# Both output projections start inside the block before them, and the router's choices are made a few tiles at a time

## What is computed

```python
# layer 0: all 1280 tokens; layer 1: only the latents go on after the mixer
h  = modulate(rmsnorm(x, norm_g[l,0]), shift, scale)       # six modulation rows per layer, from c and c_ctx
o  = neighbourhood_attention(h)  if l == 0 else  rglru_mixer(h)      # both end in "@ w_o + b_o"
x  = x + gate * (o @ w_o + b_o)                            # the projection
h2 = modulate(rmsnorm(x, norm_g[l,1]), shift2, scale2)
# hier_moe(h2): group logits (4), top 1; expert logits (8 in the group), top 2; softmax weights;
# 32 experts with SwiGLU of width 512; weighted sum over the two experts of each token
x  = x + gate2 * hier_moe(h2)
```

## Time and profile before

| | us |
|---|---|
| median of 3 runs (lowest, highest) | 2957.16 (2955.74, 2960.85) |
| the profiled execution | 2956.72 |
| its span, first to last instruction | 2954.9 |
| PE busy | 2611.4 (88%) |
| PE weight loads busy | 1813.8 (61%) |
| DVE, ACT, POOL busy | 1068.0, 859.6, 478.5 |

### The profile page before, as it was taken

How to read it: one execution, slowest core, us unless ns; L and a number is a source line. 1 busy time by engine, 2 the same in 40 slices (tenths; PEclk the granted TensorE clock), 3 DMA queues, 4 the chain that set the end, 5 groups by cost and what they waited for, 6 DMA issues and landing times. The chain is left out here.

```text
span 2954.9 us, 68818 instructions
## 1 busy us (share of the span) xinstructions
PE 2611.4 (88%) x28080; PEld 1813.8 (61%) x28081; DVE 1068.0 (36%) x2350; ACT 859.6 (29%) x1860; POOL 478.5 (16%) x590
## 2 busy tenths in 40 slices
PE   7999999999879749999999489999859599999990
PEld 6787778787635437777777344454425477777770
DVE  3233333434434322222222546556453322222225
ACT  3222322222300013333333424333400033333333
POOL 0111111111211012222222300000011022222222
PEclk9999999999979879999999589999979699999995
DMA  6323223222273467999999510000072699999995
GB/s 247 114 91 115 92 98 128 78 94 85 94 258 104 152 266 314 417 416 397 416 416 360 203 58 29 28 28 28 0 258 86 267 361 417 416 417 416 416 389 178
DMA packets 145570, 646.14 MB, mean 219 GB/s; under 512 B 33632, under 2 KB 45920, under 8 KB 89520
## 3 DMA queue, kind: packets, MB, share of 16 engines
q1 hardware_dynamic: 107600, 541.50, 46.6%
q0 software_dynamic: 17984, 57.16, 5.6%
q10 hardware_dynamic: 19872, 45.84, 4.1%
HBM read 579.86 MB, written 64.57 MB: 218 GB/s over the span
## 5 line engine op out<-in xcount | busy, mean ns | idle before, releaser
L1247 PE MATMUL PS<-wt,xT 128*32 128x256 f32 x13056 | 751.5, 381 | 32.6 <-DVE xT L1414 19.8
L1247 PEld LDWEIGHTS PS<-wt,xT 128*32 128x32 f32 x13056 | 512.5, 110 | 232.1 <-issue 41.0
L1262 PE MATMUL PS<-wt,hidT 128*32 128x256 f32 x6528 | 395.2, 379 | 3.5 <-ACT y L1155 3.5
L1155 ACT ACTIVATE y<-PS 32x256 f32<-32x256 f32 x816 | 306.3, 375 | 304.2 <-PE PS L1262 296.9
L1414 DVE STREAM_TRANSPOSE xT<-xg 128x256 f32<-128x256 f32 x206 | 91.8, 446 | 670.9 <-PE PS L1247 653.6
L1262 PEld LDWEIGHTS PS<-wt,hidT 128*32 128x32 f32 x6528 | 256.6, 110 | 99.5 <-issue 4.4
L691 PE MATMUL PS<-hT,slab 128*128 128x256 f32 x1280 | 297.1, 386 | 9.1 <-DVE low L589 6.3
L691 PEld LDWEIGHTS PS<-hT,slab 128*128 128x128 f32 x1280 | 240.5, 193 | 46.4 <-DVE low L589 8.3
L399 POOL TENSOR_SCALAR prob<-prob,inv 128x640 f32<-128x640 f32 (+2 forms) x80 | 130.4, 1629 | 677.4 <-DVE inv L604 677.4
L1100 POOL DMA_INDIRECT xg<-h_d,ib x212 | 208.3, 983 | 171.6 <-POOL ib L1097 171.6
L484 ACT ACTIVATE prob<-prob,low 128x640 f32<-128x640 f32 (+2 forms) x160 | 117.5, 735 | 293.5 <-DVE low L589 286.8
(11 more groups left out here) (228 smaller groups left out, 2580.3 us busy)
## 6 DMA issues: line engine op xcount, KB each, us to landing
wt<-in_w SPq DMA_DIRECT2D x256, 1024.0 KB, 19.4
wt<-in_w2s SPq DMA_DIRECT2D x128, 1024.0 KB, 18.6
aw<-in_ada_w SPq DMA_DIRECT2D x48, 1024.0 KB, 5.0
ys_d<-y ACTq DMA_DIRECT2D x204, 128.0 KB
slab<-in_slabs SPq DMA_DIRECT2D x24, 512.0 KB, 3.4
tab<-in_tables SPq DMA_DIRECT2D x8, 1408.0 KB, 6.8
ys_d<-zero POOLq DMA_DIRECT2D x4, 2560.0 KB, 11.4
x_d<-x_p ACTq DMA_DIRECT2D x18, 512.0 KB, 5.0
```

Source lines behind the costliest of these rows:

```text
L1155: ins = a.activation(y[rows, q * QD:q * QD + QD], PS[STRIP * q:STRIP * q + STRIP, DOWN, 0:QD], ACT.Copy)
L1247: mm = t.matmul(PS[32 * g:32 * g + 32, UP, 0:QD], xT[:, k * 32:k * 32 + 32], wt[b][:, q, c * 1024 + g * QD:c * 1024 + g * QD + QD], start= ...
L1262: mm = t.matmul(PS[32 * g:32 * g + 32, DOWN, 0:QD], hT_[:, k * 32:k * 32 + 32], wt[b][:, q, c * 1024 + g * QD:c * 1024 + g * QD + QD], sta ...
```

## The change

`projection` becomes a class `Projection` whose parts are called from the attention's and the recurrent layer's block, so two blocks go. Its loops are written out. Its tensors get fixed places, so that its loads can land while the mixer still runs. In outline:

- SP loads `w_o` (four DMAs of 1 MB) at the start of the last head pair (attention), or after the last y product (recurrent). A few steps later come the rows, x and the router's weights, which now lie contiguous in HBM, as one DMA.
- PE computes tiles 0 and 1 without their last k-slice before the mixer's last result is there, in attention between `turn`, `values` and the waits of the last step, and adds the last slice when it is.
- `rows(g)` on DVE runs one step later, after `prob_T`, and `store_mod` with the bias loads moves from ACT to SP, also one step later.
- The gate is applied per half tile. DVE makes the best groups, experts and one-hots for tiles 0 to nt-5 in tile nt-3, for the next two in tile nt-2, and for the last two after the last logits (`choose`), with running sums `A2c` over the tiles.
- In experts, PE needs two products in place of `nt` + 1; the token weights are made while PE sums the indices; and layer 1's columns come as 16 rows of 512 bytes each for latents and context, turned on PE.

```diff
@@ attention, sync
+ if i == STEPS - UNITS:
+     sp.wait_ge(w_ps, NPIECE * PAIRS)
+     pr.load_weights(sp)
+ if i == STEPS - UNITS + ABUF:
+     sp.wait_ge(s_ok, STEPS - UNITS)
...
+     pr.load_first(sp)
...
+ if made is not None:
+     store_mod(made)
+     made = None
...
+ sp.wait_ge(s_ok, STEPS)
+ pr.load_shift(sp)
...
+ sp.wait_ge(on_ok, STEPS)
+ pr.stream(sp)
@@ attention, scalar
- elif n % KD == KD - 1:
-     store_mod(n // KD)
+ pr.scalar(a)
@@ attention, vector
  prob_T(i - 1)
+ if made is not None:
+     rows(made)
+     made = None
  if i < STEPS:
      norm(i)
@@ attention, tensor, after the steps
+ pe.wait_ge(low_ok, 2 * STEPS)
+ pr.weights_ready(pe)
+ pr.part(pe, 0, 0, 0, KD - 1)
+ turn(STEPS - 1)
+ pr.part(pe, 0, 1, 0, KD - 1)
+ values(STEPS - 1)
+ pr.part(pe, 1, 0, 0, KD - 1)
+ pe.wait_ge(on_ok, STEPS)
+ pr.part(pe, 0, 0, KD - 1, KD)
+ pr.part(pe, 0, 1, KD - 1, KD)
+ pr.part(pe, 1, 0, KD - 1, KD)
+ pr.part(pe, 1, 1, 0, KD)
+ pr.rest(pe)
@@ class Projection
+ def part(self, t, n, h, lo, hi):
+     if lo == 0 and n >= 2:
+         t.wait_ge(self.sum1_ok, 3 * (n - 2) + h + 1)
+     for k in range(lo, hi):
+         mm = t.matmul(PS[:, self.banks[n % 2] + h, :], self.Z[:, k, n * P:(n + 1) * P],
+                       self.wo[:, k, h * 512:(h + 1) * 512], start=(k == 0), stop=(k == KD - 1))
...
+ def rest(self, t):
+     H = KD // 2
+     self.part(t, 2, 0, 0, KD)
+     self.turn(t, 0)
+     self.part(t, 2, 1, 0, H)
+     self.route(t, 0)
+     self.part(t, 2, 1, H, KD)
+     self.turn(t, 1)
+     self.part(t, 3, 0, 0, KD)
+     self.route(t, 1)
+     for n in range(2, self.nt):
+         if n > 2 and n + 1 < self.nt:
+             self.part(t, n + 1, 0, 0, KD)
+         if n + 1 < self.nt:
+             self.part(t, n + 1, 1, 0, H)
+         self.turn(t, n)
+         if n + 1 < self.nt:
+             self.part(t, n + 1, 1, H, KD)
+         self.route(t, n)
@@ Projection.vector
+ for n in range(nt):
+     gate(n)
+     if n == 0:
+         for w in range(W):
+             prepare(w)
+     added(n)
...
+     elif n > 2:
+         logits(n - 1)
+     normed(n)
+     if n == 2:
+         logits(1)
+     if n == nt - 3:
+         choose(0, nt - 4)
+     if n == nt - 2:
+         choose(nt - 4, nt - 2)
+ logits(nt - 1)
+ choose(nt - 2, nt)
@@ recurrent, sync
+ sp.wait_ge(u_ps, 2 * LB)
+ sp.wait_ge(y_ps, 2 * LB)
+ pr.load_weights(sp)
+ sp.wait_ge(u_ok, 2 * LB)
+ pr.load_first(sp)
@@ recurrent, tensor, after the loop
+ pr.weights_ready(t)
+ t.wait_ge(y2_ok, 2 * LB + 1)
+ t.wait_ge(z_ok, 2 * LB)
+ pr.part(t, 0, 0, 0, KD - 1)
+ pr.part(t, 0, 1, 0, KD - 1)
+ t.wait_ge(tr_ok, 4 * LB + 1)
+ pr.part(t, 1, 0, 0, KD - 1)
+ pr.part(t, 1, 1, 0, KD - 1)
+ t.wait_ge(z_ok, 2 * LB + 1)
+ for n in range(2):
+     for h in range(2):
+         pr.part(t, n, h, KD - 1, KD)
@@ experts, scalar (layer 0)
- a.dma_start(scol[:, w, :], mod_d[w, ...].rearrange("(k p) -> p k", p=P)).then_inc(cols_in, 16)
- a.dma_start(gcol[:, w, :], mod_d[w, ...].rearrange("(k p) -> p k", p=P)).then_inc(cols_in, 16)
+ a.dma_start(y[2 * KD * w:2 * KD * (w + 1), 0:P], mod_d[w, ...].rearrange("(m p) -> m p", p=P)
+             ).then_inc(cols_in, 16)
@@ experts, tensor
- t.matmul(PS[:, 0, 0:w], ltri[:, :], flat(A2), start=True, stop=False)
- for k in range(nt):
-     mm = t.matmul(PS[:, 0, (k + 1) * EXPERTS:w].rearrange(...), ones[:, :], expand(A2[:, k, :], ...), ...)
+ t.matmul(PS[:, 0, 0:w], ones[:, :], flat(A2c), start=True, stop=False)
+ t.matmul(PS[:, 0, 0:w], ltri[:, :], flat(A2), start=False, stop=True).then_inc(summed, 1)
+ if not last:
+     t.wait_ge(cols_in, 48)
+     t.matmul(PS[:, 5, 0:4 * KD], y[0:4 * KD, 0:P], ident[0:4 * KD, 0:4 * KD], start=True, stop=True
+              ).then_inc(turned, 1)
@@ experts, vector
- v.wait_ge(e_ok, 2)
- link(v.tensor_reduce(gsum, m4, AX, ALU.add))
...
  link(v.tensor_scalar(blk, PS[:, 0, nt * EXPERTS:(nt + 1) * EXPERTS], 1.0 / STRIP, 31.0 / 64, ALU.mult, ALU.add))
...
+ v.wait_ge(e_ok, 2)
+ link(v.tensor_reduce(gsum, m4, AX, ALU.add))
...
  v.wait_ge(summed, 4)
```

More of the change, by code:

```diff
@@ new lines, in attention @@
+                put = Place(nc, PROJ_AT, TOP)
+                early = [put(f"{x}0", [P, w]) for x, w in (("qT", N), ("kT", N), ("V", N))]
+                tab0 = put("tab0", [P, 2, TABW])
+                slab = [put(f"slab{m}", [P, KD, P]) for m in range(3)]
+                qT, kT, Vf = ([x, put(f"{y}1", [P, N])] for x, y in zip(early, ("qT", "kT", "V")))
+                V = [x[:, :].rearrange("p (t c) -> p t c", c=P) for x in Vf]
+                tab = [tab0, put("tab1", [P, 2, TABW])]
+                prob = [put(f"prob{b}", [P, 2, 640]) for b in range(2)]
@@ L283, in attention @@
+                low, sums, inv = (put(x, [P, 2, 2]) for x in ("low", "sums", "inv"))
+                bq = put("bq", [P, 3, PAIRS])
+                zero, cl_ok = put("zero", [P, QD]), gather_sem("ys_cleared")
                 diag = [qT[0][:, j * P:(j + 1) * P] for j in range(2)]
@@ L753, in fill @@
                                     piece(n, i)
-                        for i in range(STEPS + 1):
-                            if i < STEPS:
-                                scores(i)
+                        for i in range(STEPS):
+                            scores(i)
                             if i:
@@ L1005, in experts @@
             nm = lambda s: sem(f"{s}_m{l}")
-            dv, d_ok, e_ok, a_ok, cn_ok, z_ok, t_ok, g_ok, b_ok, o_ok, i_ok = (
-                nm(x) for x in ("dve", "diff", "exp", "assigned", "counts", "order", "tables", "later", "bases", "hot", "index"))
+            dv, e_ok, summed, masks = (nm(x) for x in ("dve", "exp", "summed_on_pe", "masks_made"))
             tab_ok, idx_ok, pad_ok = nm("tab"), nm("idx"), nm("pad")
@@ L1769, in _ @@
                             gates(b, 1, 1)
-        def weights_in(l):
-            return [[sem(f"w{b}{q}_m{l}") for q in range(NCH)] for b in range(WBUF)]
-        with ExitStack() as att:
-            OT = sbuf(att, "OT", [P, KD, N])
-            with ExitStack() as sth:
-                hT = sbuf(sth, "hT", [P, KD, N])
-                attention(hT, OT)
-            semaphores_rest()
-            w_in = weights_in(0)
-            projection(0, NT, OT, A["na_w_o"][0], A["na_b_o"][0], RLs, w_in)
@@ new lines, in _, with weights_in @@
+                        t.wait_ge(ti_ok, 4 * LB + 1)
+                        pr.rest(t)
+        def weights_in():
+            return [[root.enter_context(nc.semaphore(f"w{b}{q}")) for q in range(NCH)] for b in range(WBUF)]
+        hT, OT = at("hT", MODS_AT, [P, KD, N]), at("OT", OT_AT, [P, KD, N])
+        w_in = weights_in()
+        attention(hT, OT, Projection(0, NT, OT, A["na_w_o"][0], A["na_b_o"][0], w_in, (0, 2), 6), w_in)
+        semaphores_rest()
+        zT, hT = at("zT", MODS_AT, [P, KD, L]), at("hT1", SCR_AT, [P, KD, N])
```

631 lines of the change are left out of this document (322 added, 309 removed).

## The result

The kernel after takes 2862.05 us, the median of 4 runs (2860.85 to 2864.9), against 2958.02 us for the kernel before on the same chip (2955.74 to 2960.85). The ratio is 0.9677, with a 95% interval from 0.966 to 0.9693. The prediction was 2856 us, 6 us too low, within its range of 2843 to 2880.

The account below looks back on a forecast made before the run. PE was taken as busy in the expert stages, so gains lay in its waits between them. Terms 11.6 + 1.3 + 19.1 + 2.4 + 25.4 + 34.4 + 2.7 + 4.3 gave 101.2 us, hence 2856 us, range 2843 to 2880.

Parts of the forecast that it names:

- Group ends: Attention, four modulation group ends: PE's waits cost 12.8 us, 0.3 us left per end, so 11.6 us gained.
- Steps 78 and 79: End of attention: step 78's product ends 2.3 us earlier, less 1 us for half clock; 1.3 us gained.
- Into projection(0): From step 78's product to projection(0)'s last product: PE never idle, 180.5 us becomes 161.4; 19.1 us gained.
- Last tiles: Last product to logits in each projection: half the gate done early, DVE starts at once; 2.4 and 2.7 us gained.
- Routing of layer 0: Logits to PE's first item: exponentials no longer behind slow DMA issues, columns 2 us late; 66.0 becomes 40.6, 25.4 us gained.
- Into projection(1): After the recurrent layer: early w_o and partial products fill PE's 29.07 us idle, tile 0 2 us late; 34.4 us gained.
- Routing of layer 1: Logits to PE's first item in layer 1: 41.0 us becomes 36.6; 4.3 us gained.
- 1: Layer 0 routing: small column DMAs wait behind 12 MB of weights, 22 us lost, 2876 us; chance 0.08.
- 2: Expert stages: weights become the bound, 5 to 10 us in each layer, 2866 to 2876 us; chance 0.08.
- 3: Attention keeps its stalls: bias rows delay norm and POOL, SP's store delays slab loads, 6 us each, 2868; chance 0.06.
- rival 4: Projections' DVE and ACT: late instructions in straight-line code lengthen a tile's 7.0 us chain, kernel slower, 2973 at 16; chance 0.01.
- 5: Both projections: PE cannot start before zT or OT is complete, 24 and 14 us come back, 2894; chance 0.02.

Follow-up runs that it names:

- run 4: The kernel before with ACT's five column DMAs of layer 0's experts moved behind the two exponentials: 2935.75 us, against 2957.26 for the kernel before in that series.
- run 2: The kernel after with the store and the next bias loads back on ACT, still one step late: 2863.42 us.
- run 5: The kernel after with layer 0's columns turned on PE behind the index sums instead of ahead of the tables' products: 2859.8 us.
- run 6: The kernel after with DVE preparing the projection's rows ahead of the first gate: 2854.45 us.
- run 9: The kernel after with all tiles' experts chosen behind the last logits, the running sums kept: 2870.82 us.
- runs 1 to 9: The first nine follow-up runs, all edits of the kernel after except run 4: 2854.45 to 2935.75 us.
- run 7: The kernel after without partial products ahead of the mixer's last result, loads still early: 2881.72 us.
- runs 11: Run 10's kernel with products nobody reads filling PE's waits around the routing and ahead of the first u product: 2903.86 us.
- run 12: The kernel with those idle products plus 11 tiny products at the start of PE's stream, moving later code by 44 records: 2831.46 us.
- run 10: The kernel after with columns turned behind the index sums, rows prepared ahead of the first gate, and tile 0's first partial product inside step 79: 2847.86 us.

## Why the prediction was right, and where its terms were off

The forecast came true by its mechanism, but not in every term. On the profiled executions it promised 101.2 us, and 91.8 came. The rows that fell short make 12.6 us; 3.3 more than forecast came in the others, most of it in attention, and of that up to 2.5 us is luck of the two executions.

**Group ends, 11.6 forecast, 12.8 measured** (11.0 against the trace of run 4). The mechanism held: rows in front of the masked adds and the store in front of the exponentials. The residual of 0.3 us per end does not exist. The prediction did not tell the two parts apart; the runs do: 6.4 us are DVE's order, 4.9 more come with the store in the same step, and of the store only the time mattered, not the engine (2).

**Steps 78 and 79, 1.3 forecast.** The product of step 78 ends 3.1 us earlier after the start of its head pair (2.3 forecast). The half clock behind it costs 8.79 - 6.17 = 2.6 us where 1 was taken, from bounds of 0 and 3: the near end was chosen and the far one came. In the other traces of the same code it is 1.2 to 2.7.

**Into projection(0), 19.1 forecast.** 180.5 - 164.5 is 16.0, and the half clock is inside it. With these 2.6 us and the 1.0 us that PE waited for tile 0 put back, it is 19.6, for the 19.1 of the working: the sum of PE's pieces was right, and what was off are the clock, sized at 1 in place of 2.6, and tile 0, sized at nothing. "Moving the rows' preparation behind the first gate costs nothing" was wrong: it held POOL's first addition back, and beside POOL DVE was slower. PE's 1.03 us wait for tile 0 is also over the limit of 1 us that the prediction set.

```profile
825.30 1.22 DVE L933 TENSOR_TENSOR bg_p<-gt_p,bo_p 128x1024 f32<-128x1024 f32 x1
...
826.69 6.45 POOL L891 TENSOR_TENSOR xt_p<-xt_p,bg_p 128x1024 f32<-128x1024 f32 x2 [25.48 <-DVE bg_p L933]
827.57 3.37 DVE L933 TENSOR_TENSOR bg_p<-gt_p,bo_p 128x1024 f32<-128x1024 f32 x1
```

These are three rows of the kernel after: the same instruction of DVE takes 1.22 us before POOL starts and 3.37 beside it.

**Last tiles, 2.4 and 2.7 forecast, 2.5 and 2.8 measured.** The chain of half gates, addition, root and logits came out at 13.5 us for the 13.6 of the working.

**Routing of layer 0, 25.4 forecast, 22.3 measured.** By pieces: logits to the first product 6.2 us (5.9), to DVE's first table instruction 2.8 (3.3), and from there to the first item 34.8, where 29.4 and 2 for late columns were taken. The last of the three loads landed 8.7 us after the block's start (8.1 taken from the gather's row), beyond the 8 us that the prediction named as a sign of being wrong. It cost 3.8 us, not 2, because DVE's masks were ready earlier than put; run 5 shows the 3.8. The two new loads alone, there by 5.7 us, would hardly have been late: it was `ncol`, a load that the kernel before had too. The other 1.6 us is the index sums, 8.02 us for the 6.39 of before at another granted clock; "then unchanged" left the clock out. That part is this execution's: the same sums took 6.38 us in run 2. Run 4 puts 21.5 us on the queue order alone, the largest piece of this row, and it is right.

The prediction weighed the Trainium skill (DMA: Bandwidth & Descriptors, Issuing engines are not separate DMA queues), whose rule is that the issue time one saves is usually small relative to the DMA itself. Run 4 decides for the row: one issue took 20.04 us, and taking it and its four neighbours from in front of the exponentials gave 21.5. In the kernel before, these column loads took 15.5 to 33.9 us from issue to landing, so an issue of 18.15 was not small beside them. For ordinary issues the rule holds: run 2 moved eight of them, 2.38 us, for nothing.

**Into projection(1), 34.4 forecast, 28.9 measured.** Gates' end, start of the partial products and `zT` came as said. The failed step is the sentence "DVE has tile 0 ready only at 2174.7: 2 us". The wait was 4.5, since the working put POOL's addition and DVE's at the durations they have alone, and the half clock behind the wait, (1.97 - 1.04) + (5.43 - 3.60) = 2.8 us, was not in the sum. 2.5 + 2.8 is 5.3 of the 5.5 us that are missing, and run 6 takes all 4.5 + 2.8 = 7.3 away.

**Routing of layer 1, 4.3 forecast, 4.1 measured.** Right. "Choosing the last tiles last saves little" was not: run 9 puts 7.5 us on it in both layers by PE's waits, 8.8 by the medians. With the running sums in the choice the number of instructions does depend on the number of tiles, and the wider ones take longer too. The sentence did not enter the sum, which took the last choice at 5.5 us and measured 5.6.

**The stretch in between** is 1.7 us longer after. It spans the first layer's experts and the recurrent block. The same code took 1058.3 to 1059.8 us there in the traces of runs 1 to 9, and 0.8 of the 1.7 us is the first item, 6.13 us for 5.30 at a lower granted clock; the rest was not looked into further.

**The rivals.** 1: the columns came late by 3.8 us, not by 22. 2: no wait for weights; the stages keep 5.2 us per item. 3: no group end is left. 4: a tile's chain on DVE is 6.3 us, not longer than before, and the straight-line code of DVE and ACT shows no wait for instructions. 5: its prices were wrong. It said that without early partial products 24 and 14 us come back; run 7 measured 17.0 and 1 to 3. In layer 0 the working took PE's own products for a gap that they would fill, but PE was not idle there: what was gained in layer 0 is then left to the loads and the block boundary, which no run takes apart. That rival had 2 in 100 and decided nothing, but it would have been wrong by 18 us.

## What to carry to other kernels

Before costing a moved instruction at nothing, look at what stands behind it in the queue of every engine that waits for it: 21.5 of these 96 us were two exponentials behind slow issues, and 7.6 more were to be had from one preparation in front of a gate. Early loads paid most (34.8 us in layer 1); early products paid only for the time in which PE would have stood (17.0 us there, 1 to 3 in layer 0). Where PE waits, read the granted clock behind the wait and add what it costs, and after any edit to PE's code compare the packets of its instruction loads.

## What had not been expected of the hardware

**Code position.** 72.4 us hung on where a loop of PE lay (runs 11 and 12): 58.8 us of waits stand against 6.8 in run 12's stage, and behind them the clock was lower. The waits show as "issue", with no releaser, 13 of them of up to 7.6 us, and the instruction queue had 142 packets in place of 86. The Trainium skill (Advanced Engine Details and Errata, ISA Cache) gives cache lines of 16 KB, 256 instructions, and 128 KB on TensorE, from which eight lines would follow. The same list says that there are only two lines; with two, this loop would have loaded code in every turn of every kernel, and in run 10 its second turn moved no packet. The trace agrees with the size of a line: 16.4 KB per packet, and 8 packets more for each turn. A loop of 1536 records and a few dozen others is just over six lines long and touches seven or eight, according to where it starts; that eight is the case in which it reloads all of them is my reading of these counts, and the runs show one bad position beside the good ones of all the others, layer 1's loops among them. The prediction's rival 4 looked for this cost on DVE and ACT, in straight-line code; it was on PE, in a loop.

**The clock.** Around PE's waits the granted clock fell, to half behind the 4.50 us at 2117, but also at 801 us behind three waits of 2.6 us together, and idle products in the waits kept it up: from 955 us to about the first item it was 0.64 in run 10 and 0.94 in run 12:

```profile
955.00:1016.00 61.00, 28.14 (x242) 20.46 (x244) 28.10 (x98) 3.96 (x6) 5.09 (x10) 0.64 0.58 238
```

```profile
955.00:1011.00 56.00, 49.52 (x367) 36.90 (x369) 27.57 (x94) 3.96 (x6) 5.36 (x11) 0.94 0.58 235
```

The first line is run 10's, the second run 12's. Work that nobody reads was worth 16.4 us.
